# Modulation row sums of the first feed-forward taken from single partial results, with two of eight products on ScalarE

## The reference, cut to what matters

```python
cs = jax.nn.silu(c)
for layer in range(DEPTH):
    mod = cs @ mod_w[layer] + mod_b[layer]          # mod_w[layer]: 1024 x 6144
    sh1, sc1, g1, sh2, sc2, g2 = jnp.split(mod, 6, axis=-1)
    ...
    h = modulate(rms_norm(x, norm_g[layer, 1]), sh2, sc2)
    x = x + g2[:, None, :] * conv_ffn(h, ...)
def conv_ffn(h, w_up, w_gate, dw_w, dw_b, w_down):
    g = causal_dwconv(h @ w_gate, dw_w, dw_b)       # 3 taps
    return (jax.nn.silu(g) * (h @ w_up)) @ w_down
```

## Time and profile before

| | |
|---|---|
| median of 3 runs | 1572.63 us (1568.77 to 1572.94) |
| profiled execution | 1573.68 us, of which the span is 1571.9 us |
| PE / DVE / ACT busy | 1463.6 / 1207.0 / 756.6 us |
| DMA | 314.72 MB, mean 200 GB/s |
| granted clock of TensorE, mean | 0.97 of full |

### The profile page before, as it was taken

One profiled execution on the slowest core, in us unless ns is written; L12 is line 12 of the kernel. 1 busy time (PEld: TensorE's weight loads), 2 busy tenths in 40 slices (PEclk: granted clock), 3 DMA queues, 4 the chain that ended last, 5 costly groups with the idle time before them and its releaser, 6 DMA issues.

```text
span 1571.9 us, 26257 instructions
## 1 busy us (share of the span) xinstructions
PE 1463.6 (93%) x9806; PEld 1244.4 (79%) x9820; DVE 1207.0 (77%) x1895; ACT 756.6 (48%) x1080; POOL 51.5 (3%) x38
## 2 busy tenths in 40 slices
PE   5598989999999899999989889999999999999998
PEld 2484468999978666999979765689998787799997
DVE  7998747999989947799995557576667768776666
ACT  3322356444454525544436567565555632365544
POOL 2501100000000000000000100000000000000000
PEclk7798999999999989999998999999999999999999
DMA  9333836878846554988853510335455433354551
GB/s 363 136 109 127 328 148 248 341 295 316 335 162 270 214 196 179 391 331 317 336 194 124 162 40 1 116 141 212 169 182 199 164 118 134 115 175 172 183 197 69
DMA packets 57320, 314.72 MB, mean 200 GB/s; under 512 B 6902, under 2 KB 8159, under 8 KB 33119
## 3 DMA queue, kind: packets, MB, share of 16 engines
q1 hardware_dynamic: 53272, 302.40, 51.2%
q10 hardware_dynamic: 3974, 11.33, 2.2%
HBM read 310.98 MB, written 1.15 MB: 199 GB/s over the span
## 4 chain that ended last, share of the span: by engine, by line
PE 71%; DVE 14%; ACT 6%; issue 5%; DMA 3%; ACTq 0%; DVEq 0%; POOL 0%; SPq 0%
PE bank L2090 58%; DVE w_lo L1213 2%; PE bank L2335 2%; ACT w_hi L691 2%; DMA raw<-in_stream 1%; PE bank L2349 1%; PE bank L2370 1%; PE bank L1976 1%; DVE hf L1426 1%; DVE arena L1251 1%; PE bank L1994 1%; ACT arena L1007 1%; DVE x L1432 1%; ACT hf L1130 1%; PE bank L2158 1%
## 5 line engine op out<-in xcount | busy, mean ns | idle before, releaser
L2090 PE MATMUL bank<-h_hi,w_hi 128*128 128x256 f32 x1928 | 554.7, 288 | 17.2 <-DVE h_lo L1414 15.6
L2090 PE MATMUL bank<-h_lo,w_hi 128*128 128x256 f32 x1928 | 547.7, 284 | 0.0
L2090 PE MATMUL bank<-h_hi,w_lo 128*128 128x256 f32 x1928 | 547.6, 284 | 0.0
L1213 DVE TENSOR_TENSOR w_lo<-raw,w_hi 128x2048 fp32r<-128x2048 f32 x186 | 426.2, 2292 | 135.7 <-ACT w_hi L691 134.5
L691 ACT ACTIVATE w_hi<-raw 128x2048 fp32r<-128x2048 f32 x186 | 355.9, 1915 | 133.0 <-PE bank L2090 74.9
L2090 PEld LDWEIGHTS bank<-h_hi,w_hi 128*128 128x128 f32 x1928 | 372.0, 193 | 19.0 <-DVE h_lo L1414 9.6
L2090 PEld LDWEIGHTS bank<-h_lo,w_hi 128*128 128x128 f32 x1928 | 372.2, 193 | 2.1 <-issue 0.7
L2090 PEld LDWEIGHTS bank<-h_hi,w_lo 128*128 128x128 f32 x1928 | 372.1, 193 | 0.0
L1629 DVE SCALAR_TENSOR_TENSOR arena<-bank,par,arena 128x255 f32<-128x255 f32 (+1 forms) x264 | 109.1, 476 | 109.9 <-ACT arena L921 77.5
L2090 PE MATMUL bank<-w_hi,a_hi 128*128 128x512 f32 x368 | 145.9, 396 | 7.1 <-DVE a_lo L1654 6.2
L2090 PE MATMUL bank<-w_hi,a_lo 128*128 128x512 f32 x368 | 145.0, 394 | 0.0
(11 more groups left out here) (299 smaller groups left out, 1774.9 us busy)
## 6 DMA issues: line engine op xcount, KB each, us to landing
raw<-in_stream SPq DMA_DIRECT2D x186, 1024.0 KB, 4.9
arena<-in_mod_stream SPq DMA_DIRECT2D x64, 768.0 KB, 6.3
arena<-in_mod_later SPq DMA_DIRECT2D x48, 512.0 KB, 5.7
raw<-in_mod_pe SPq DMA_DIRECT2D x36, 512.0 KB, 6.2
arena<-in_mod_pe SPq DMA_DIRECT2D x12, 512.0 KB, 12.2
sq<-row_store ACTq DMA_DIRECT2D x7, 512.0 KB, 3.7
sq<-in_bias SPq DMA_DIRECT2D x8, 256.0 KB, 6.6
x<-in_x_t ACTq DMA_DIRECT2D x1, 1024.0 KB, 8.8
```

The costliest lines, as they stand in the source:

```text
L1213: nc.vector.tensor_tensor(w_lo[s][:], raw[s][:], w_hi[s][:].bitcast(F32), ALU.subtract).then_inc(lo_done, 1)
L2090: ins = nc.tensor.matmul(out_, l, r, start=first and n == 0, stop=last and n == 2, **kw)
```

## The change

On DVE, the first two of the eight products of every block (row tiles 0 and 1) are dropped; ACT makes them, as two `activation(Copy, scale=...)` of 128 x 384, in a new function `mod_begin`. DVE's first operation of a block waits for it. Every block moves one place ahead, on both engines: block 0 (and 16) stands ahead of the loop, and the places in the loop hold what was one later; nothing stands behind the loop any more. This is done in both feed-forwards. The diff shows in turn `mod_begin` and its places (ACT), `mod_block` and its places (DVE), `rows_out` and `columns_out` (DVE), and PE's side.

In `ffn(0)` alone the sum over the partitions has another form. The finished block is now the moving operand: three matmuls of 128 columns, whose stationary operand is 128 x 32 and has ones in a single column, so that block b is added to row 32g+b of one PSUM bank (`mod_sum`). They stand behind up(2i+1), down(2i) and up(2i+2), and that of block 15 ahead of down(10). PE's loop is written out for this in `ffn(0)` (five turns). Then DVE adds a bias in rows (`rows_out`) ahead of `x_add`, PE transposes the rows to columns behind down(10) (`columns_turn`), DVE copies them behind `x_add` (`columns_out`), and ACT stores the rows with three DMAs and no copy. `rows_turn(1)` and `mod_out` for this layer go away. A new load (128 x 192 floats: the picking columns and the bias) is issued on ACT's queue behind `store_rows(0)`.

```diff
+            def mod_begin(b, i=None):
+                per = 0 if i is None else i
+                buf, landed, n, _ = MOD_HALF[2 * b]
+                act.wait_ge(landed, n + 16 * per)
+                if b < MOD_BLOCKS:
+                    if b >= len(mod_acc):
+                        act.wait_ge(sem("mod_turned"), b - len(mod_acc) + 1 + 3 * per)
+                else:
+                    act.wait_ge(sem("mod_used"), MOD_SLOTS + 2 * (b - len(mod_acc)) + 2 + 6 * per)
+                for e in range(2):
+                    ins = nc.scalar.activation(mod_parts(b, per)[e], buf[:, e, :], ACT.Copy, scale=silu_c[:, c0 + e:c0 + e + 1])
+                ins.then_inc(sem("mod_begun"), 1)
...
+                if b0 is not None:
+                    mod_begin(b0)
-                    run(2 * i + 1, q0 + 2, q0 + 5, i)
-                    run(2 * i + 2, q0 + 5, q0 + 8, i)
+                    run(2 * i + 1, q0 + 2, q0 + 5, i, {0: 1, 2: 2})
+                    run(2 * i + 2, q0 + 5, q0 + 8, i, {0: 3})
...
-                for kt in range(DT):
+                for kt in range(2, DT):
+                    if kt == 2:
+                        dve.wait_ge(sem("mod_begun"), b + 1 + 3 * per)
-                    if kt < 2:
-                        ins = nc.vector.tensor_scalar(parts[e], w, c, None, ALU.mult)
...
+                if b0 is not None:
+                    mod_block(b0, c0)
-                    run(2 * i + 1, q0 + 2, q0 + 5, i, {0: 0, 2: 1})
-                    run(2 * i + 2, q0 + 5, q0 + 8, i, {0: 2})
+                    run(2 * i + 1, q0 + 2, q0 + 5, i, {0: 1, 2: 2})
+                    run(2 * i + 2, q0 + 5, q0 + 8, i, {0: 3})
-                if b0 is not None:
-                    mod_block(b0 + 15, c0)
+                if f == 0:
+                    rows_out(f)
...
+            def rows_out(r):
+                dve.wait_ge(sem("mod_turned"), MOD_BLOCKS * (r + 1))
+                dve.wait_ge(sem("row_stored"), ROW_STORED[2 * r])
+                nc.vector.tensor_tensor(mod_rows[:], bank[6][0:96, 0:P], row_bias[0:96, :], ALU.add).then_inc(sem("gates_known"), 1)
+
+            def columns_out(r):
+                dve.wait_ge(sem("rows_turned"), 2 * r + 2)
+                l = (1, 4)[r]
+                nc.vector.tensor_copy(mod[:, l, 0:48].rearrange("p (b g) -> p g b", g=3),
+                                      bank[7][:, 0:96].rearrange("p (g b) -> p g b", g=3)[:, :, 0:MOD_BLOCKS]).then_inc(sem("gates_known"), 1)
+                dve.wait_ge(sem("gates_known"), 4 + 2 * r)
...
+            def mod_sum(b, r):
+                pe.wait_ge(sem("mod_used"), MOD_SLOTS + 2 * (MOD_BLOCKS * r + b) + 2)
+                for g in range(3):
+                    ins = nc.tensor.matmul(bank[6][32 * g:32 * g + 32, 0:P], pick[:, 31 - b:63 - b],
+                                           mod_acc[b % len(mod_acc)][:, 0, g * P:(g + 1) * P],
+                                           start=False, stop=b == MOD_BLOCKS - 1, skip_group_check=True)
+                ins.then_inc(sem("mod_turned"), 1)
...
+                        q += 6 * i
+                        up_gate(s, q)
+                        mod_sum(3 * i + 2 * e, f)
+                        down(s - 1, q + 2)
+                        if not e:
+                            mod_sum(3 * i + 1, f)
+                if b0 is None:
+                    with pe.Fori(0, 5) as i:
+                        two_steps(i)
+                else:
+                    for i in range(5):
+                        two_steps(i)
+                    mod_sum(MOD_BLOCKS - 1, f)
                 down(10, q0 + 32, last=True)
                 if b0 is not None:
-                    mod_turn_now(b0 + 15, 45)
+                    columns_turn(f)
```

More of the change, by code:

```diff
@@ L200, in laid_out @@
     out["rows"] = np.stack([w["cm_b_out"][0], w["final_g"], w["hy_b_out_2"][0], w["final_g_2"]])
+    picks = np.zeros((P, 64 + P), np.float32)
+    picks[:, 31] = 1
+    cols = w["mod_b"].reshape(-1, P)[48:].reshape(MOD_BLOCKS, 3, P)
+    for g in range(3):
+        picks[32 * g:32 * g + MOD_BLOCKS, 64:] = cols[:, g]
+    out["mod_pick"] = picks
     out["ctx_t"] = tiled(w["ctx_2"][0].T).reshape(P, -1)
@@ L319, in build, with mod_parts @@
         mod_keep = at(MOD_KEEP, MOD_BLOCKS * MOD_COLS)
+        def mod_parts(b, per):
+            part = mod_acc[b % 3]
+            if b < MOD_BLOCKS:
+                return [part[:, 0, :], part[:, 1, :]]
+            return [mod_keep[:, bass.ds(b % MOD_BLOCKS * MOD_COLS + 3 * MOD_COLS * per, MOD_COLS)], part[:, 1, :]]
+        pick, row_bias = at(ARENA - 512, 64), at(ARENA - 448, P)
         both_wide = at(MOD_KEEP + MOD_BLOCKS * MOD_COLS, DT, 32)
@@ L738, in store_rows @@
                 l, n, b = ROWS[i]
+                if i == 1:
+                    act.wait_ge(sem("gates_known"), 3)
+                    for g in range(3):
+                        act.dma_start(row_store[i, 0:n * P].rearrange("(b g p) -> g b p", g=3, p=P)[g], mod_rows[32 * g:32 * g + MOD_BLOCKS, :])\
+                            .then_inc(sem("row_stored"), 16)
+                    return
                 act.wait_ge(sem("rows_turned"), i + 1)
                 if i:
-                    act.wait_ge(sem("row_stored"), 16 * i)
+                    act.wait_ge(sem("row_stored"), ROW_STORED[i - 1])
                 nc.scalar.activation(mod_rows[0:n, :], bank[b][0:n, 0:P], ACT.Copy).then_inc(sem("rows_copied"), 1)
-                act.wait_ge(sem("rows_copied"), i + 1)
+                act.wait_ge(sem("rows_copied"), max(i, 1))
                 act.dma_start(row_store[i, 0:n * P].rearrange("(j p) -> j p", p=P), mod_rows[0:n, :]).then_inc(sem("row_stored"), 16)
@@ L907, in filter_hidden, with ffn @@
                 nc.scalar.activation(hid[n], angle[0], ACT.Sin).then_inc(sem("hy_hid"), 1)
-            def ffn(f):
+            def ffn(f, b0=None, c0=0):
                 last, two = f == LAST_FFN, f >= 2
@@ L945, in slot_hi, with run @@
                     return a_hi[:, k:k + 2, :]
-                def run(s, q, nq, i=None):
+                def run(s, q, nq, i=None, blocks={}):
                     g = step(s, q, i)
@@ L952, in run @@
                             hi(nq + k, i)
+                        if b0 is not None and k in blocks:
+                            mod_begin(b0 + blocks[k], i)
                 g = step(0, q0)
@@ L972, in ffn @@
                 nxt[0] = q0 + 35
-            ffn(0)
+            ffn(0, MB[1], 0)
             def later_copy(g):
@@ L1023, in _ @@
             store_rows(2)
-            ffn(1)
+            ffn(1, MB[4], 8)
             norm_x(BOTH)
@@ L1227, in mod_block @@
                 per = 0 if i is None else i
[L1228 to L1235, removed]
+                parts = mod_parts(b, per)
                 last = [None, None]
-                for kt in range(DT):
+                for kt in range(2, DT):
                     kh, e = kt // 4, kt % 2
                     buf, landed, n, _ = MOD_HALF[2 * b + kh]
-                    w = buf[:, kt % 4, :]
-                    c = silu_c[:, c0 + kt:c0 + kt + 1]
-                    if kt % 4 == 0:
+                    if kt == 2:
+                        dve.wait_ge(sem("mod_begun"), b + 1 + 3 * per)
+                    if kt == 4:
                         dve.wait_ge(landed, n + 16 * per)
-                    if kt < 2:
-                        ins = nc.vector.tensor_scalar(parts[e], w, c, None, ALU.mult)
[L1246 to L1252, removed]
+                    if kt == 5:
+                        dve.wait_ge(sem("mod_used"), MOD_SLOTS + 2 * b + 1 + 6 * per)
+                    elif kt > 3:
+                        chain_wait(last[e])
+                    ins = nc.vector.scalar_tensor_tensor(parts[e], buf[:, kt % 4, :], silu_c[:, c0 + kt:c0 + kt + 1], parts[e], ALU.mult, ALU.add)
+                    if kt == 3:
                         ins.then_inc(sem("mod_used"), 1)
-                        last[e] = None
                     else:
@@ L1350, in _, with mod_out @@
             dve.wait_ge(sem("powers_ready"), 1)
-            def mod_out(l, b, name, first=0, last=48, src=6):
+            def mod_out(l, b, name):
                 dve.wait_ge(sem("mod_turned"), b)
-                bias = par[:, COL[name] + 48 + first:COL[name] + 48 + last]
-                nc.vector.tensor_tensor(mod[:, l, first:last], bank[src][:, first:last], bias, ALU.add).then_inc(sem("gates_known"), 1)
-                dve.wait_ge(sem("gates_known"), 3 + (l == 4))
+                bias = par[:, COL[name] + 48:COL[name] + 96]
+                nc.vector.tensor_tensor(mod[:, l, 0:48], bank[6][:, 0:48], bias, ALU.add).then_inc(sem("gates_known"), 1)
+                dve.wait_ge(sem("gates_known"), 5)
+            def rows_out(r):
[8 more added lines that the diff above has]
+                dve.wait_ge(sem("gates_known"), 4 + 2 * r)
             def first_mod_out(g0, g1):
@@ L1700, in ffn @@
```

(33 more changed lines are left out.)

13 lines of the change are left out of this document (8 added, 5 removed).

## The result

| | before | after |
|---|---|---|
| median of 13 runs | 1572.94 us (1568.77 to 1577.59) | 1563.99 us (1558.11 to 1572.93) |
| ratio, 95% interval | | 0.9941 (0.9929 to 0.9953) |
| profiled execution, span | 1573.68, 1571.9 us | 1564.22, 1562.4 us |
| PE / DVE / ACT busy | 1463.6 / 1207.0 / 756.6 us | 1463.0 / 1187.0 / 787.0 us |

1563 us was forecast. The ratios in this document leave out two slow executions, one of 5004.59 us (e1) and one of 1846.12 us (the kernel before, beside e1 to e4).

The account below looks back on a forecast made before the run. PE was taken to bound the turns, so DVE relief counts only where PE waits. Terms summed to -9.95 us against 1573.68, hence 1563.7 (1562.7 against the median); 1563 us was forecast, range 1556 to 1569.5.

Parts of the forecast that it names:

- start of `ffn(0)`: Start of ffn(0): PE idles 1.5 us for block 1 behind down(0) and goes on 1.35 us later.
- 13 sums: Between down(1) and the end of down(9): each sum 0.40 us instead of 0.56, -2.1 us (from -4.0 to +2.5).
- end of `ffn(0)`, `x_add`: End of ffn(0): x_add waits for the last conversion, no longer for a block, -4.2 us.
- end of `ffn(1)`: End of ffn(1): x_add 5.6 us earlier; PE's gap before the transposing from 3.32 to about 1.6 us.
- Blocks and products: Inside turns: block 3.77 us, ACT product 0.55, DVE at 30.3 and 31.1 us a turn, PE's bound unchanged.
- Rival (b): Sums in ffn(0) dear, each 0.75 us: 4.6 us back, 1567.5 us; chance 0.12.
- (c): Sums at 0.25 us, no half clock at ffn(0)'s start or behind ffn(1): 1559 us or little less; chance 0.12.
- Written out code: PE's loop in ffn(0) written out as straight code: priced at 0.
- PE's gap is all but gone: End of ffn(0): a_lo ends 1.6 us earlier, so PE's 1.55 us gap and the half clock behind it go.
- (d): One end's gain is lost to another wait, PE reaching a late chunk or load: 1568 to 1570 us; chance 0.07.
- (e): Inside turns: halves come late and eat the slack, slower, +17 us (1580) at 22 us landings; chance 0.05.
- (f): Whole kernel: nothing shows, half clocks and gaps move rather than vanish, 1570 to 1573 us; chance 0.04.

Follow-up runs that it names:

- e1: Kernel before with only two of eight products moved to ACT, blocks and sums at old places in old form: 1567.5 us, 0.9974.
- e4: Full change without ACT's products: all eight on DVE, blocks one place ahead, new sums, PE's loop written out: 1572.22 us, 0.9997.
- e5: Kernel before with only PE's loop of ffn(0) written out: 1575.74 us in a single execution.
- e9: Kernel before with only the new form of sums in ffn(0), at old places, all products on DVE: 1571.92 us, 0.9999.
- e11: Same kernel as e6 (full change, sums at old places), measured again beside e10 and e12: 1560.64 us, 0.9927.
- e12: Same kernel as e3 (products on ACT, blocks one place ahead, old sums), measured again: 1559.3 us, 0.9918.
- e10: The full change measured once more, beside e11 and e12: 1564.31 us, 0.9951.
- e6: Full change with the sums at their old places, that of block 15 still ahead of down(10): 1559.98 us, 0.9912.
- e7: e6 with the first chunk of the convolution's weights (cm_in) loaded ahead of six other pieces: 1561.23 us, 0.9918.
- e8: e3 with the first chunk of cm_in loaded ahead of six other pieces: 1560.44 us, 0.9916.
- e3: Kernel before with products on ACT and blocks one place ahead, old sums and PE's loop kept: 1560.14 us, 0.9925.
- e2: Kernel before with only the blocks one place ahead, all eight products on DVE, old sums: 1567.51 us, 0.9964.

## Why the prediction was right, point by point

The mechanism held: nothing was won inside the turns but the sums' small part, and nearly all came from the two ends. The sum was -9.95 us; the two profiled executions differ by 9.5, the medians by 8.95. That it came so close is partly luck: 1.35 us that no term had stand against terms that were 0.8 to 1.2 us too dear. Term by term:

| term | predicted | measured | from |
|---|---|---|---|
| before `ffn(0)` | 0 | +1.35 | start of the stage, table above; it varies that much by itself |
| start of `ffn(0)` | +1.35 | +1.7 | PE goes on at 281.04, 36.2 us into the stage; before 278.00, 34.5 |
| half clock behind it | +0.8 | 0 | clock 1.00 for the 3.5 us behind the gap of 1.52 us |
| 13 sums | -2.1 | -1.6 | 13 x 0.12 |
| end of `ffn(0)`, `x_add` | -4.2 | -4.3 | 170.55 to 164.64 us from the start's gap to `x_add` is -5.9; less the sums |
| transposing behind it | 0 | +0.55 | 452.73-445.68 = 7.05; before 6.5 |
| start of `ffn(1)` | +1.0 | near 0 | PE waits 0.2 us for `w_lo` |
| end of `ffn(1)` | -5.6 | -5.35 | `x_add` 190.5 us into the stage; before 195.85; the row above is in it |
| half clock behind it | -1.2 | -2.4 | 3.77 us from the transposing to the next stage (821.76-817.99); before 6.2 |

Added up, the column of measured terms gives -10.05 us. The stage behind `ffn(1)` gave some 0.6 of it back: it is 1.8 us shorter and not 2.4.

- **Blocks and products.** As worked out: 3.77 us a block, 0.55 a product. DVE is at 30.68 and 31.29 us a turn (30.3 and 31.1). The work taken from DVE inside a turn bought nothing there, but e4 shows what the shorter block is worth at the edges: without it new sums and places together gain nothing (0.9997), with it 0.6%. Its worth is not its 0.66 us; it is whether PE stands still.
- **The sums** were mis-sized in two ways that offset each other. They take 0.35 us and not 0.40, but the piece behind each is 0.09 longer: net 0.44 against 0.56. Rival (b), 0.75 each, falls, and so do the sums of 0.25 in (c); the other two parts of (c), no half clock at the start and none behind `ffn(1)`, came true. e5 rules out the written out loop as the cause of the 0.09. By the Trainium skill (TensorEngine Tiling (Array Packing), Tiling Modes), a change of mode drains the engine. The trace agrees in so far as there is a cost of 0.09 us; that it is such a drain no run shows. In the time of the whole this term can't be seen (e9, e11 with e12), so of the -9.95 it is the one that only traces support.
- **Written out code.** Priced 0, and e5's chain shows 0 inside a turn.
- **The start of `ffn(0)`** was the right cost, read as unavoidable. It isn't a cost of the places of the blocks: in e12, with the same blocks one place ahead, PE has no wait for a block, since the sum stands one piece of the chain later. It belongs to the early sums, which the prediction took from the diff without asking what they cost. By the medians they cost 3.7 us. The waits for blocks (1.8 us in e10, none in e11) are the part that the traces show. `ffn(0)` is 1.0 us longer in e10 than in e11, which has the longer gap ahead of down(10), and 2.6 longer than in e6. Of the 3.1 us between the profiled executions of e10 and e11, 2.5 lie in the stage behind, 165.5 against 163.0 us. The clock is not the cause, its mean is 0.97 in both: PE waits some 2.6 us more there in e10, most of it for one tile of ACT (e10, then e11):

```profile
PE bank L2427 <- ACT arena L1020: 9.3, 5, 4.9
```
```profile
PE bank L2427 <- ACT arena L1020: 7.7, 5, 4.7
```

That the early sums bring this about is not shown.
- **The end of `ffn(0)`** came to -3.7 in place of -4.2. The step "PE's gap is all but gone" failed here: 1.14 us stayed, for a chunk that came late. In e10's trace the gap is 0.7 us, in e11's 2.0, behind a landing of 14.70 us. The later the chunk, the longer the gap (see e7), but loading it sooner gained nothing that e7's or e8's medians show.
- **The end of `ffn(1)`** was right in place and size for `x_add`, but both of PE's gaps were mis-sized: the one for `a_lo` is 2.15 us and not near 1, the one before the transposing 0.56 and not 1.6. Of the 2.4 us behind it half was counted, and all of it came back. Each half of the change helps one engine only. The shorter blocks bring `a_lo` forward (gap 2.15 in e1), but block 31 still holds `x_add`: PE waits 4.3 us before the transposing, with a clock of 0.58 behind that gap. The new places free `x_add`, but the gap for `a_lo` stays at 3.5 (clock 0.71 behind it), and PE itself comes late to the transposing. In e12, with both, the gaps are 2.15 and 0.6, at full clock. The transposing needs both engines, and that is why the feed-forwards of e3 and e12 gain more than those of e1 and e2 together.
- **Rivals (d), (e) and (f)** are ruled out: both ends gained, no wait for a landing shows on DVE inside the turns, and the interval ends at 0.9953. A small piece of (d) is there, the 0.55 us that the late chunk costs at the end of `ffn(0)`.

## What to carry over

Shorten a side engine's work for the places where the main engine waits for it, and count those, not the busy time. Let the consumer ask late: shorter blocks one place ahead gained 0.8%, and moving their consumer ahead with them gave a third of that back. When a step needs two engines, and each of two edits speeds up one of them, measure the edits together, since either alone leaves the other engine late.

## What was unexpected of the hardware

**The same gap is followed by half clock in one execution and not in another.** One place in the convolution has a gap of 1.96 or 1.97 us in all fourteen traces, with the same matmuls behind it. Five are followed by half clock (before, after, e1, e3, e5) and nine are not, and after and e10 are one kernel. Before, after and in e10 (busy time by stretch, 3.5 us from the end of the gap):

```profile
578.39:581.89 3.50, 3.50 (x9) 2.81 (x10) 1.03 (x2) 3.04 (x4) 0.00 (x0) 0.54 0.11 46
```
```profile
576.22:579.72 3.50, 3.50 (x9) 2.85 (x10) 1.03 (x2) 3.04 (x4) 0.00 (x0) 0.57 0.22 88
```
```profile
576.07:579.57 3.50, 3.50 (x16) 2.95 (x16) 1.02 (x2) 3.03 (x4) 0.00 (x0) 1.00 0.21 84
```

The clock is 0.54 and 0.57, 9 matmuls in 3.5 us, against 1.00 and 16. Likewise a gap of 3.46 us for `a_lo` at the end of `ffn(1)`: half clock in e9, full in e4.

```profile
804.91:808.41 3.50, 3.50 (x8) 2.78 (x9) 3.50 (x5) 1.02 (x2) 0.00 (x0) 0.50 0.00 0
```
```profile
811.76:815.26 3.50, 3.50 (x15) 2.90 (x16) 3.43 (x4) 1.02 (x2) 0.00 (x0) 1.00 1.03 400
```

Gaps of 1.54, 1.55, 2.00 and 2.33 us (e2, before, twice e4) were followed by it, ones of 1.52 (twice), 1.80 (e5), 1.97 (e11) and 2.01 us (e9) were not. At the end of `ffn(1)`, gaps of 2.15 or 2.16 us were followed by it twice (e3 0.63, e7 0.51) and seven times not, e12 among them, which is the kernel of e3. So the length of a gap between 1.5 and 3.5 us does not decide it alone; what else does stays open. It explains much of the spread between executions: the convolution, with the same code in both, takes 161.43 us at a mean clock of 0.99 in e6 and 165.61 at 0.96 after, though PE waits nearly the same in it (7.4 and 7.7 us for one tile of ACT, 2.0 for another). Not all of it is clock, as e10 and e11 show above. A single profile's total can't settle a term of 2 us. The length of its own stage, with clock and waits beside it, says more, though that too differs by 1.5 us between e6 and e11, which are one kernel.
